# First loads in another order and on another queue, and a final norm whose sums come out by token

## The reference, cut to what matters

```python
def rms_norm(x, g):
    xf = x.astype(jnp.float32)
    y = xf * lax.rsqrt(jnp.mean(xf * xf, axis=-1, keepdims=True) + EPS)
    return (y * g.astype(jnp.float32)).astype(x.dtype)

# beginning: layer 0 of the first model
h = rms_norm(x, mix_norm[0])
u = h @ w_in                                   # (512, 1024) @ (1024, 2048)
gate_branch, x_branch = jnp.split(u, 2, axis=-1)
xc = causal_depthwise_conv(x_branch, conv_w, conv_b)
r = sigmoid(blockwise(xc, w_r) + b_r); i = sigmoid(blockwise(xc, w_i) + b_i)
...
# end: after layer 1 of the second model, h is (528, 1024)
return rms_norm_2(h, final_norm_g)[:, N_META:, :]   # (512, 1024)
```

## Time and profile before

| | us |
|---|---|
| three timed runs, median (lowest, highest) | 3097.01 (3094.31, 3097.84) |
| the profiled execution's own time | 3099.01 |
| its span, first to last record | 3096.8 |
| TensorE matmul busy | 2999.5 (97%) |
| VectorE, ScalarE, GpSimd busy | 1796.2, 650.6, 412.7 |
| DMA, mean over the span | 68 GB/s |

### The profile page before, as it was taken

The page is one execution under the profiler, slowest core; times in us unless marked ns, Lnnn a source line. Parts: engine busy times, 40 slices in busy tenths (PEclk is TensorE's granted clock), DMA queues, the critical chain, the costliest instruction groups (busy, mean ns, idle before and its releaser), DMA issues.

```text
span 3096.8 us, 42240 instructions
## 1 busy us (share of the span) xinstructions
PE 2999.5 (97%) x18070; PEld 2550.5 (82%) x18070; DVE 1796.2 (58%) x2345; ACT 650.6 (21%) x1186; POOL 412.7 (13%) x390
## 2 busy tenths in 40 slices
PE   6989999999999999989989999999999999999998
PEld 5878888888778888878778878888888777888887
DVE  4656645455566653532566667887555134888754
ACT  1311100021431100002336531211010164111201
POOL 2112210120001210020023300111110011111101
PEclk9999999999999999999999999999999999999999
DMA  4222231322102223121100022223222100222320
GB/s 121 68 65 85 82 108 56 96 69 69 41 28 82 82 82 109 55 82 43 61 1 4 4 91 82 82 82 102 75 82 82 55 1 25 67 91 90 102 75 28
DMA packets 207574, 209.48 MB, mean 68 GB/s; under 512 B 8997, under 2 KB 206333, under 8 KB 207389
## 3 DMA queue, kind: packets, MB, share of 16 engines
q1 hardware_dynamic: 207356, 206.76, 20.9%
q10 hardware_dynamic: 32, 0.03, 0.0%
HBM read 204.65 MB, written 2.10 MB: 67 GB/s over the span
## 4 chain that ended last, share of the span: by engine, by line
PE 90%; DVE 5%; ACT 2%; issue 1%; POOL 1%; SPq 1%; DMA 0%; POOLq 0%; DVEq 0%; ACTq 0%
PE pp L272 57%; PE pp L149 15%; PE pp L1201 4%; PE pp L2678 2%; PE pp L2658 1%; PE pp L1966 1%; PE pp L1313 1%; PE pp L1949 1%; PE pp L1625 1%; DVE arena L348 1%; PE pp L1921 1%; PE pp L2707 1%; PE pp L1336 1%; PE pp L2329 1%; DVE rs L823 1%
## 5 line engine op out<-in xcount | busy, mean ns | idle before, releaser
L272 PE MATMUL pp<-arena 128*128 128x264 f32 (+1 forms) x8400 | 1853.3, 383 | 10.5 <-DVE arena L329 6.8
L272 PEld LDWEIGHTS pp<-arena 128*128 128x128 f32 x8400 | 1594.8, 190 | 267.7 <-DVE arena L329 8.8
L149 PE MATMUL pp<-arena 128*128 128x256 f32 (+5 forms) x2144 | 480.4, 384 | 9.7 <-DVE arena L1047 8.0
L149 PEld LDWEIGHTS pp<-arena 128*128 128x128 f32 (+4 forms) x2144 | 398.3, 187 | 88.0 <-issue 14.5
L832 POOL TENSOR_TENSOR sq<-sq 128x512 f32<-128x512 f32 (+1 forms) x48 | 80.6, 1679 | 751.0 <-ACT sq L812 747.7
L360 ACT COPY arena<-pp 128x528 f32<-128x528 f32 (+1 forms) x60 | 34.9, 582 | 612.8 <-PE pp L272 545.4
L348 DVE TENSOR_TENSOR arena<-arena 128x256 f32<-128x256 f32 (+5 forms) x176 | 152.7, 890 | 6.1 <-POOL arena L2559 2.4
L2485 ACT ACTIVATE arena<-arena,par 128x528 f32<-128x528 f32 x88 | 68.1, 821 | 385.8 <-DVE arena L2516 385.8
L2559 POOL TENSOR_TENSOR arena<-arena 128x528 f32<-128x528 f32 x44 | 72.1, 1638 | 494.5 <-DVE arena L2528 494.5
L1201 PE MATMUL pp<-arena 128*128 128x256 f32 (+1 forms) x576 | 125.8, 380 | 0.0
L1171 POOL TENSOR_TENSOR arena<-arena 128x1024 f32<-128x1024 f32 x32 | 83.4, 2608 | 316.4 <-ACT arena L1119 273.2
(11 more groups left out here) (290 smaller groups left out, 2900.6 us busy)
## 6 DMA issues: line engine op xcount, KB each, us to landing
arena<-in_mlp_w_dram SPq DMA_DIRECT2D x64, 1024.0 KB, 5.5
arena<-in_ffn_up_dram SPq DMA_DIRECT2D x44, 1024.0 KB, 5.1
arena<-in_ffn_down_dram SPq DMA_DIRECT2D x16, 1408.0 KB, 7.3
arena<-in_fox_w_in_dram SPq DMA_DIRECT2D x12, 1024.0 KB, 5.3
arena<-in_lru_w_in_dram SPq DMA_DIRECT2D x8, 1024.0 KB, 7.0
arena<-in_lru_w_out_dram SPq DMA_DIRECT2D x4, 1024.0 KB, 5.2
arena<-in_fox_w_out_dram SPq DMA_DIRECT2D x4, 1024.0 KB, 5.3
arena<-in_rw_wk_dram SPq DMA_DIRECT2D x4, 1024.0 KB, 7.6
```

Of the source, the lines that this page charges most:

```text
L149: mm = pe.matmul(bank[0:m, h, 0:r.shape[1]], slot[0:kp, kk, j * P:j * P + m], r, start=kt == 0, stop=kt == nk - 1)
L272: return pe.matmul(k.pp[seventh(k, name, n, i) % NB][:, j, 0:hw], stationary[i][:, kk, j * P:(j + 1) * P], moving[i][:, kk, :], start=kk = ...
```

## The change

- SyncE no longer waits for a cleared `prow`. It issues input and meta tokens first, then the first four weight units, then (after the block weights were cleared) the block weights, the other groups of parameter rows and the small vector, then the rest of the weight units.
- The first group of rows is issued by ScalarE, ahead of all its other work, once `prow` was cleared. It has a semaphore of its own.
- TensorE turns this group alone at first. It turns the four other groups after the product `lru_x` (`turn_other_rows`), into a tile that ScalarE copies.
- ScalarE copies all eight channel tiles of the input.
- In the last norm GpSimd adds one square fewer. TensorE uses the squares as stationary operand with four columns of ones moving, 4 token blocks for each of three buffers, so that a token's sum lies on its partition. ScalarE takes the root of 128x4 numbers, VectorE the reciprocal; `turn_roots` and `keep_roots` go. The table with the root is loaded ahead of the first square.
- ScalarE scales blocks 0 and 2, VectorE 1 and 3. Blocks are stored in the order 0, 1, 2, 3.

```diff
@@ block.sync
             load_inputs(sp, k)
-            load_weights(sp, k)
+            load_weights(sp, k, 0, RING)
+            load_later_inputs(sp, k)
+            load_weights(sp, k, RING, len(k.weights.units))
@@ block.scalar
+            act.wait_ge(k.made, 1)
+            load_rows(act, k, True)
             for s in stages:
@@
-def load_inputs(sp, k):
-    sp.wait_ge(k.made, 1)
+def load_rows(eng, k, first):
+
     for c in k.param_copies:
+        if (c[0] == 0) != first:
+            continue
+        landed = k.rows_landed if first else k.rest_landed
...
+def load_inputs(sp, k):
     for t in range(4):
         sp.dma_start(k.xrow[:, t, :], k.A["x"][0, t * P:(t + 1) * P, :]).then_inc(k.loaded, 16)
     sp.dma_start(k.mrow[0:META, :], k.A["meta_tokens_2"]).then_inc(k.loaded, 16)
-    sp.dma_start(k.small[0:HEADS, 48:49], k.A["fox_b_f"].rearrange("a n -> n a")).then_inc(k.loaded, 16)
+def load_later_inputs(sp, k):
     sp.wait_ge(k.made, 2)
...
+    load_rows(sp, k, False)
+    sp.dma_start(k.small[0:HEADS, 48:49], k.A["fox_b_f"].rearrange("a n -> n a")).then_inc(k.rest_landed, 16)
@@ def stage_turn_inputs(k):
-    k.psum.add("x_in", ["dve", "act"] * (KT // 2))
+    k.psum.add("x_in", ["act"] * KT)
...
-        e.wait_ge(k.loaded, 16 * (len(k.param_copies) + 6))
         e.wait_ge(k.made, MADE)
-        for t in range(5):
-            mm = e.transpose(k.pp[gp % NB][:, t // 4, (t % 4) * P:(t % 4 + 1) * P], k.prow[:, t, :], k.ident[:, :])
-        mm.then_inc(k.full, 1)
+        e.wait_ge(k.rows_landed, 16 * sum(c[0] == 0 for c in k.param_copies))
+        e.transpose(k.pp[gp % NB][:, 0, 0:P], k.prow[:, 0, :], k.ident[:, :]).then_inc(k.full, 1)
+        e.wait_ge(k.loaded, 16 * 5)
...
+def turn_other_rows(pe, k):
+    g = k.psum.base["params_rest"]
+    take(pe, k, g)
+    pe.wait_ge(k.rest_landed, 16 * (sum(c[0] > 0 for c in k.param_copies) + 1))
+    for t in range(1, 5):
+        mm = pe.transpose(k.pp[g % NB][:, 0, (t - 1) * P:t * P], k.prow[:, t, :], k.ident[:, :])
+    mm.then_inc(k.full, 1)
@@ def stage_scale(..., last=False): act
+            if last and f == 0:
+                e.preload_act_table_set("sqrt_and_others")
             e.activation(k.sq[:, f % 2 if f else 2, 0:W], k.x[:, f, t0:TOK], ACT.Square).then_inc(k.sq_ready, 1)
-        if not square and not late:
+        if not square and not late and not last:
             root(e, k, name)
@@ pool
-        for f in range(1, KT - 1):
+        for f in range(1, KT - 2 if last else KT - 1):
@@ def stage_lru(k): pe, act
         product(e, k, "lru_x", h_tile(k, t0), h_wait(e, k, hb))
+        turn_other_rows(e, k)
...
+        filled(e, k, g)
+        freed(k, g, e.copy(k.par[:, P:5 * P], k.pp[g % NB][:, 0, :]))
@@ def stage_store(k): pe
-            sum_squares(e, k, norm)
+            n = k.norms[norm][0]
+            p = k.psum.base["out_sums"]
+            take(e, k, p)
+            for i, j in enumerate((2, 0, 1)):
+                if j == 2:
+                    e.wait_ge(k.sq_added, 6 * k.norm_order[norm] + 5)
+                else:
+                    e.wait_ge(k.sq_ready, KT * n + KT - 1 + j)
+                for t in range(4):
+                    mm = e.matmul(k.pp[p % NB][:, 0, 4 * t:4 * t + 4], k.sq[:, j, META + t * P:META + (t + 1) * P],
+                                  k.ones[:, 0:4], start=i == 0 and t == 0, stop=i == 2, skip_group_check=True)
+            mm.then_inc(k.full, 1)
         for t in range(4):
-            if norm and t == 2:
-                e.wait_ge(rooted, 1)
-                turn_roots(e, k, "out_roots", rspans)
...
@@ act, dve, sync
+            freed(k, p, e.activation(by, k.pp[p % NB][:, 0, 0:16:4], ACT.Sqrt, bias=k.small[:, 40:41], scale=1.0 / D))
+            e.wait_ge(rooted, 1)
-        for t in range(2):
+        for t in (0, 2):
...
-            keep_roots(e, k, "out_roots", rspans)
-            was_read(e, k, k.psum.base["out_roots"])
-        for t in range(2, 4):
+            was_read(e, k, k.psum.base["out_sums"])
+            e.reciprocal(by, by).then_inc(rooted, 1)
+            e.wait_ge(rooted, 1)
+        for t in (1, 3):
...
-        for t in (0, 2, 1, 3):
+        for t in range(4):
```

More of the change, by code:

```diff
@@ L580, in __init__ @@
         self.pe, self.act, self.dve, self.pool, self.sync = pe, act, dve, pool, sync
-def load_inputs(sp, k):
-    sp.wait_ge(k.made, 1)
+def load_rows(eng, k, first):
     for c in k.param_copies:
+        if (c[0] == 0) != first:
+            continue
+        landed = k.rows_landed if first else k.rest_landed
         if len(c) == 4:
             t, r, m, src = c
-            sp.dma_start(k.prow[r:r + m, t, :], src).then_inc(k.loaded, 16)
+            eng.dma_start(k.prow[r:r + m, t, :], src).then_inc(landed, 16)
         else:
             t, r, m, src, h = c
-            sp.dma_start(k.prow[r:r + 1, t, h * HD:(h + 1) * HD], src).then_inc(k.loaded, 16)
+            eng.dma_start(k.prow[r:r + 1, t, h * HD:(h + 1) * HD], src).then_inc(landed, 16)
+def load_inputs(sp, k):
     for t in range(4):
@@ L601, in load_inputs, with load_weights @@
                          k.A[name][0].rearrange("(f h) d e -> h d f e", h=2)[h]).then_inc(k.wri_loaded, 16)
-    k.n_loaded = 16 * (len(k.param_copies) + 6)
-def load_weights(sp, k):
-    for u, (copies, _) in enumerate(k.weights.units):
+    load_rows(sp, k, False)
+    sp.dma_start(k.small[0:HEADS, 48:49], k.A["fox_b_f"].rearrange("a n -> n a")).then_inc(k.rest_landed, 16)
+def load_weights(sp, k, first, last):
+    for u in range(first, last):
+        copies, _ = k.weights.units[u]
         if u in k.hold:
@@ L715, in dve @@
         filled(e, k, gp)
[L716 to L720, removed]
+        freed(k, gp, e.tensor_copy(k.par[:, 0:P], k.pp[gp % NB][:, 0, 0:P]))
+        was_read(e, k, gp)
         filled(e, k, gm)
@@ L725, in act @@
         e.wait_ge(k.made, MADE)
-        for f in range(1, KT, 2):
+        for f in range(KT):
             filled(e, k, gx + f)
@@ L780, in root, with stage_scale @@
                                scale=1.0 / D))
-def stage_scale(k, gains, t0, outs=None, square=False, late=False):
+def stage_scale(k, gains, t0, outs=None, square=False, late=False, last=False):
     n = k.n_norm
@@ L819, in dve @@
                 scale(e, f)
+        if last:
+            return
         if name in k.first_sums:
@@ L946, in stage_lru @@
     plan_product(k, "lru_x", w_in, [(D, 2 * D)], "dve")
+    k.psum.add("params_rest", ["act"])
     k.psum.add("lru_ri", ["act"] * (2 * KT))
@@ L2924, in stage_store @@
     norm, k.norm_due = k.norm_due, None
-    rspans = [(META + t * P, META + (t + 1) * P) for t in range(4)]
     if norm:
[L2927 to L2934, removed]
+        k.psum.add("out_sums", ["act"])
+    k.psum.add("out", ["act", "dve", "act", "dve"])
     g = k.psum.base["out"]
@@ L2940, in stage_store @@
     fin = STOP is None
+    rooted = k.sem("out_rooted")
     def pe(e):
         if norm:
[L2944 to L2950 removed]
+            n = k.norms[norm][0]
[10 more added lines that the diff above has]
+            mm.then_inc(k.full, 1)
+        for t in range(4):
+            take(e, k, g + t)
             for f in range(KT):
@@ L2957, in pe @@
                     s = k.x[:, f, META + t * P:META + (t + 1) * P]
-                mm = e.transpose(k.pp[p % NB][:, f // 4, (f % 4) * P:(f % 4 + 1) * P], s, k.ident[:, :])
+                mm = e.transpose(k.pp[(g + t) % NB][:, f // 4, (f % 4) * P:(f % 4 + 1) * P], s, k.ident[:, :])
             mm.then_inc(k.full, 1)
-    rooted = k.sem("out_rooted")
     def act(e):
         if norm:
-            was_read(e, k, k.psum.base["out_roots"])
-        for t in range(2):
-            p = g + at[t]
+            p = k.psum.base["out_sums"]
@@ L2973, in act @@
-            freed(k, p, op)
+                op = e.copy(halves(orow[:, t, :]), k.pp[(g + t) % NB][:, :, :])
+            freed(k, g + t, op)
     def dve(e):
         if norm:
-            e.memset(k.small[:, 56:57], 0.0).then_inc(rooted, 1)
-            keep_roots(e, k, "out_roots", rspans)
-            was_read(e, k, k.psum.base["out_roots"])
-        for t in range(2, 4):
-            p = g + at[t]
-            filled(e, k, p)
+            was_read(e, k, k.psum.base["out_sums"])
+            e.reciprocal(by, by).then_inc(rooted, 1)
@@ L3043, in plan @@
     if STOP is None:
-        st.append(stage_scale(k, ["final_norm"], 0))
+        st.append(stage_scale(k, ["final_norm"], 0, last=True))
     st.append(stage_store(k))
```

17 lines of the change are left out of this document (10 added, 7 removed).

## The result

| | before | after |
|---|---|---|
| median of the timed runs, us | 3095.66 (4 runs) | 3073.94 (4 runs) |
| lowest, highest | 3092.84, 3097.84 | 3072.77, 3074.30 |
| profiled execution, its span | 3099.01, 3096.8 | 3073.82, 3071.8 |

A forecast was written before the change was run, and what follows sets the result against it. TensorE, busy 2999.5 of 3096.8 us, was taken as the bound, leaving chains of waits at both ends to shorten. Start 15.8 plus end 5.8 made 21.6 us, off the median 3097.0: 3075.4, range 3072 to 3083.

The forecast's parts named there:

- T: Time at which TensorE starts to transpose the input, 27.03 us before; forecast 10.4, set by the later of input and rows.
- The order: At the start: first rows expected to arrive a little later than the input, which was forecast landed at 8.95 us.
- the issue time: ScalarE's 16 issues of the first rows: 1.27 us for the first, 0.39 for each of the others.
- Landing takes 2.1 us from the issue: At the start: time from a row load's issue to its landing, taken from the smallest load in the DMA view.
- delay the input by 0.2: At the start: the 64 KB of rows, sharing the DMA engines, would hold the input up by some 0.2 us.
- The first rival: At the start: ScalarE's row issues stand in line with SyncE's weight units; T 17.3, time 3082.3 us; chance 0.22.
- The second rival: At the start: input has no precedence over the weight units behind it; T 19.4, time 3084.4 us; chance 0.07.
- From T to the scaling: Input transposes up to the first norm's scaling: 7.2 us, from 6.8 before plus 0.4 for four more slow transposes.
- From the scaling to the block product: Work here moves along with the scaling; four row transposes behind `lru_x` add 0.45 us.
- GpSimd is free: In the first norm: GpSimd's masks end by 18 us, its first add comes after 17.6, so it delays nothing.
- The end: Last norm to first store: sums by matmul, short reciprocal and no turned factors bring the store 5.8 us earlier, bounds 5.2 to 6.3.
- The sum: Whole kernel: 15.8 us from the start plus 5.8 from the end, 21.6 us in all.

The follow-up runs named there:

- rows turned late: Changed kernel, but TensorE transposes the first parameter rows behind the input's channel tiles instead of ahead of them; median 3069.2 us, ratio 0.9915 to the kernel before.
- the split by block: Kernel with rows turned late, and TensorE transposes each 128-token block of the first four channel tiles as it lands; median 3070.7 us, ratio 0.9916 to before.
- the end alone: Kernel before the change with only the changed last norm and stores; median 3090.2 us, ratio 0.9983 to before.
- The start alone: Changed kernel with the last norm and stores put back as before; median 3080.0 us, ratio 0.9950 to before.
- the late start: Changed kernel, but SyncE waits for the last of GpSimd's chunk masks before issuing the input; median 3085.0 us, ratio 0.9965 to before.
- the exchanged queues: Changed kernel, but ScalarE issues input and meta tokens, SyncE the first rows and then the weight units; median 3073.2 us, ratio 0.9924 to before.
- the units held back: Changed kernel, but SyncE waits for the first rows to land before issuing the first four weight units; median 3072.3 us, ratio 0.9927 to before.

## Why the prediction was right, and where it was not

**T, the landing of the rows: mis-sized.** The order was right (rows later than the input), and so was the issue time: ScalarE's issues took 0.29 to 0.59, the last at 7.34, where the forecast gave 8.2. The term that failed was "Landing takes 2.1 us from the issue". It was 5.8. The term came from a load with nothing beside it, and alone it is indeed 1.7. I had let the rows delay the input by 0.2, and had not asked what input and units do to them: 2.5 us from the input, 1.6 more from the units. T was 13.5, inside the range but 3.1 late.

**The first rival** (queues hold each other up) has its shadow in this, but not its mechanism: SyncE's units were held for 9.55 us, and ScalarE's issues beside them were not, 0.32 each. What waited behind the units were the packets, and beside the input the semaphore's updates, not the issues. The Trainium skill's rule, quoted with the first part, that DMAs of all issuers interleave on the same engines, agrees as far as the packets go; the 0.2 us drawn from it looked at the wrong one of the two.

**The second rival** (no precedence for the input) fell: with 4 MB behind them, input and meta tokens had landed by 9.2 (rows turned late) and 9.6 (changed). 8.95 was the forecast, with bounds of 8.0 and 9.8.

**From T to the scaling:** 7.4 in the profile of the changed kernel, forecast 7.2; but 6.1 to 7.0 in the seven other profiles without the split by block. It depends in part on when the transposes go from 0.21 to 0.11 us each: the 32 took 6.46 us here and 5.2 to 6.1 in those seven. **From the scaling to the block product:** 60.0, as before plus the 0.45 of L752; but 58.2 to 59.0 where the adds came later. "GpSimd is free" was true and beside the point: a GpSimd still busy with its masks would have been better, since its adds pace the scaling. The trace of before had it: 8.33 us for eight scalings, where the same operation in the last norm takes 0.45 (timeline of before):

```profile
3079.17 0.90 DVE L801 TENSOR_SCALAR arena<-x,par 128x528 f32<-128x528 f32 x2
```

**The end:** 5.8 forecast, 5.85 in the profile, 5.3 by the ratio of the end alone. The mechanism held in each step.

**The sum.** In the profiles the two ends give 18.3. The medians of the whole say 21.7, the ratios of the parts 15.5 + 5.3. The start alone gave 15.5 where one profile showed 12.5; its own profile shows 14.9, by a shorter way from T to the scaling (6.3 for 7.4) and from there to the block product (59.0 for 60.0). So that 21.6 came so near is partly luck: T was 3.1 late, and gains that I had not listed made up for it. The rest lies in the middle, 2976 to 2985 us in twelve profiles with the same arithmetic there, most of it where the clock fell in one execution and not in the other. That the start's place causes it is excluded by the late start only as far as one profile and five timed runs go. What makes the clock fall at those moments stays open.

## What to carry to other kernels

A small load that takes 1.7 us alone can take 4 to 6 beside large ones, on another queue too: price its landing under the load that will be there, or let nothing wait for it that doesn't need its data. Ask of each wait whether it is in the program's order only; moving one transpose behind 32 others brought the scaling 5.0 us forward, the exchanged queues 2.5 (in the profiles). Two single profiles can differ by 7 us in code that is the same, so the difference of two spans is no measure of a change at their ends.

## What the runs showed of the hardware that was not expected

- A 4 KB load from HBM took 1.7 us from issue to the release of TensorE alone, 4.2 with 2.1 MB in flight on the other queue, 5.8 with 1 MB units behind that. The 4.2 was the same on either queue; the 5.8 was measured on ScalarE's alone.
- With the units held back the DMA engines were idle from 9 us on, and the last update of the rows' semaphore still came 2.5 us behind their last packet; alone it was 0.3.
- ScalarE issues such a load in 0.32 us (its first in 0.59), SyncE in 0.295.
- A scaling of 128x512 on VectorE takes 0.41 us alone and 1.42 while GpSimd adds tiles of that size.
- TensorE's clock fell right behind the last product in 8 of 10 profiles with the new end, with TensorE waiting 0.75 us ahead of the last small matmuls (six of them) as with under 0.1 (the two that turn block 0 there). It cost the six some 0.5 to 0.9 us up to the first store.
